# A four-layer fp32 trunk: the two parts of x and h at other SBUF distances from the weights in each feed-forward phase

## The reference, cut to what matters

```python
# x: (1, 256, 1024); DEPTH = 4; D_FF = 2816; all float32
def _swiglu(h, w_gate, w_up, w_down):
    return (jax.nn.silu(h @ w_gate) * (h @ w_up)) @ w_down

for i in range(DEPTH):
    x = x + 0.5 * _swiglu(_rms_norm(x, norm_ffn1[i]), ffn1_w_gate[i], ffn1_w_up[i], ffn1_w_down[i])
    h = _rms_norm(x, norm_mix[i])
    # mixer by i % 3: forgetting attention (layers 0 and 3), a convolution module (1),
    # differential attention (2)
    x = x + y
    x = x + 0.5 * _swiglu(_rms_norm(x, norm_ffn2[i]), ffn2_w_gate[i], ffn2_w_up[i], ffn2_w_down[i])
return x
```

## Time and profile before

| what | value |
|---|---|
| time, median of 2 runs | 1983.55 us (1982.61 to 1984.5) |
| the profiled execution | 1982.23 us |
| its span | 1980.4 us |
| mean granted TensorE clock | 0.997 of 2.4 GHz |
| TensorE matmuls, weight loads | 12558, 12558 |

### The profile page before, as it was taken

The page is one execution under the profiler, slowest core; times in us unless marked ns, Lnnn a source line. Parts: engine busy times, 40 slices in busy tenths (PEclk is TensorE's granted clock), DMA queues, the critical chain, the costliest instruction groups (busy, mean ns, idle before and its releaser), DMA issues.

```text
span 1980.4 us, 29058 instructions
## 1 busy us (share of the span) xinstructions
PE 1948.2 (98%) x12558; PEld 1712.4 (86%) x12558; DVE 1423.8 (72%) x1653; ACT 1044.4 (53%) x1250; POOL 102.0 (5%) x114
## 2 busy tenths in 40 slices
PE   7999999999999998999999999999999999999999
PEld 6888889888888896988888888788888888889887
DVE  7776678875787565876587658887758765778763
ACT  6554556553555344654465455575436544566542
POOL 3000001000200002100100000010000000001000
PEclk9999999999999999999999999999999999999999
DMA  7655435655665683665666553356566656435653
GB/s 239 193 184 182 149 128 157 192 188 187 192 192 180 201 246 89 191 192 188 194 191 192 180 181 128 107 178 192 180 196 191 191 181 193 139 128 171 192 189 107
DMA packets 336365, 350.14 MB, mean 177 GB/s; under 512 B 10077, under 2 KB 331886, under 8 KB 336238
## 3 DMA queue, kind: packets, MB, share of 16 engines
q1 hardware_dynamic: 331742, 343.58, 54.5%
q10 hardware_dynamic: 4496, 4.70, 1.2%
HBM read 346.04 MB, written 2.22 MB: 176 GB/s over the span
## 4 chain that ended last, share of the span: by engine, by line
PE 91%; DVE 4%; ACT 2%; DMA 1%; issue 1%; POOL 1%; ACTq 0%; SPq 0%; DVEq 0%; POOLq 0%
PE banks L1458 49%; PE banks L1463 25%; PE banks L1449 4%; PE banks L1450 4%; PE banks L1451 4%; PE banks L1675 1%; DMA u_away<-sb_u_pad 1%; PE banks L1728 1%; ACT sb_w_high L475 1%; DVE sb_w_low L813 1%; PE banks L1695 1%; PE banks L1712 1%; PE banks L1916 1%; ACT sb_scores L603 0%; DMA sb_raw<-in_ffn_w_gate 0%
## 5 line engine op out<-in xcount | busy, mean ns | idle before, releaser
L813 DVE TENSOR_TENSOR sb_w_low<-sb_raw,sb_w_high 128x2048 fp32r<-128x2048 f32 (+1 forms) x332 | 749.9, 2262 | 211.4 <-ACT sb_w_high L475 210.6
L1458 PE MATMUL banks<-sb_x_both,sb_w_high 128*128 128x512 f32 x2816 | 720.7, 392 | 2.2 <-ACT sb_w_high L475 2.2
L475 ACT ACTIVATE sb_w_high<-sb_raw 128x2048 fp32r<-128x2048 f32 (+1 forms) x332 | 618.5, 1867 | 124.1 <-DMA sb_raw<-in_ffn_w_down 106.6
L1458 PEld LDWEIGHTS banks<-sb_x_both,sb_w_high 128*128 128x128 f32 x2816 | 498.5, 188 | 82.6 <-ACT sb_w_high L475 2.4
L1463 PEld LDWEIGHTS banks<-sb_x_both,sb_w_low 128*128 128x128 f32 x2792 | 386.1, 188 | 35.5
L1463 PE MATMUL banks<-sb_x_both,sb_w_low 128*128 128x256 f32 x2792 | 394.3, 278 | 0.0
L1458 PE MATMUL banks<-sb_h_both,sb_w_high 128*128 128x512 f32 x1408 | 360.1, 394 | 0.0
L1458 PEld LDWEIGHTS banks<-sb_h_both,sb_w_high 128*128 128x128 f32 x1408 | 250.2, 188 | 45.7
L1463 PEld LDWEIGHTS banks<-sb_h_both,sb_w_low 128*128 128x128 f32 x1408 | 190.8, 188 | 17.1
L1463 PE MATMUL banks<-sb_h_both,sb_w_low 128*128 128x256 f32 x1408 | 194.2, 278 | 0.0
L493 ACT ACTIVATE sb_x_both<-sb_xT,sb_vec 128x256 fp32r<-128x256 f32 x96 | 43.3, 500 | 199.5 <-DVE sb_xT L846 175.5
(11 more groups left out here) (232 smaller groups left out, 1931.1 us busy)
## 6 DMA issues: line engine op xcount, KB each, us to landing
sb_raw<-in_ffn_w_gate SPq DMA_DIRECT2D x88, 1024.0 KB, 5.4
sb_raw<-in_ffn_w_up SPq DMA_DIRECT2D x88, 1024.0 KB, 5.4
sb_raw<-in_ffn_w_down SPq DMA_DIRECT2D x64, 1024.0 KB, 5.0
sb_raw<-in_ffn_w_down SPq DMA_DIRECT2D x32, 768.0 KB, 4.3
sb_raw<-in_fox_w_in SPq DMA_DIRECT2D x24, 1024.0 KB, 5.2
sb_raw<-in_conv_w_pw SPq DMA_DIRECT2D x12, 1024.0 KB, 6.2
sb_raw<-in_diff_w_in SPq DMA_DIRECT2D x12, 1024.0 KB, 5.1
sb_raw<-in_fox_w_out SPq DMA_DIRECT2D x8, 1024.0 KB, 4.9
```

Source lines behind the costliest of these rows:

```text
L475: act.activation(slot(w_high, b)[:, 0:width(b)], slot(raw, b)[:, 0:width(b)], ACT.Copy).then_inc(S["high_ready"], 1)
L813: dve.tensor_tensor(slot(w_low, b)[:, 0:width(b)], slot(raw, b)[:, 0:width(b)], slot(w_high, b)[:, 0:width(b)].bitcast(F32), ALU.subtract) ...
L1458: return pe.matmul(pair(bank[at][:, :]), high[:, n * P:(n + 1) * P], m_both, start=first, stop=last, skip_group_check=True)
```

## The change

`x_both` and `shift_x` become one tensor `x_home` of 2 x 8192 + 864 bytes that begins at 114816, at distance 0 from a weight slot. `x_parts(i)` takes the two parts of phase i out of it at `X_PLACE[f]` elements (4 bytes each), f being the number of the feed-forward phase; for a mixer it takes element 16, which is the address of before. `h_both` and `shift_h` become `h_home`, whose start is the address that `h_both` had, with the parts at `H_PLACE[f]` elements from it. All readers and writers of x and h take their views from these functions.

The distances of x's high part from a weight slot, in bytes, are by feed-forward phase 32, 48, 56, 72, 80, 96, 112 and 208 (before: 64 in all). Those of h's, beyond a multiple of 1024, are 32, 48, 80, 96, 16, 160, 224 and 240 (before: 960). The low part follows the high part at 8192 and 22528 bytes, as before. By this layout none of the sixteen is a multiple of 64; two of them, x's 56 and 72, are no multiple of 16. All tensors that stand between x and h (among them the constants, the table `wide` and `gate_parts`) move up by 800 bytes. No instruction is added, removed or moved.

```diff
+X_PLACE = [8, 12, 14, 18, 20, 24, 28, 52]
+H_PLACE = [24, 28, 36, 40, 20, 56, 72, 76]
...
-        sb("shift_x", [P, 16])
-        x_both = sb("x_both", [P, 2, KT, SEQ], F32R)
-        x_high, x_low = x_both[:, 0, :, :], x_both[:, 1, :, :]
+        x_home = sb("x_both", [P, 2 * KT * SEQ + 216], F32R)
+
+        def two_parts(home, tiles, at):
+
+            return home[:, at:at + 2 * tiles * SEQ].rearrange("p (c k n) -> p c k n", c=2, k=tiles)
+
+        def x_parts(i):
+            return two_parts(x_home, KT, X_PLACE[number(i)] if phases[i] == "ffn" else 16)
...
-        sb("shift_h", [P, 200])
         with ExitStack() as during_ffn:
-            h_both = during_ffn.enter_context(nc.sbuf_tensor("sb_h_both", [P, 2, FF_TILES, SEQ], F32R))
+            h_home = during_ffn.enter_context(nc.sbuf_tensor("sb_h_both", [P, 2 * FF_TILES * SEQ + 224], F32R))
...
+        def h_parts(i):
+            return two_parts(h_home, FF_TILES, H_PLACE[number(i)])
...
             def x_highs(i, T):
...
+                x_high = x_parts(i)[:, 0, :, :]
...
             def x_lows(i, T):
...
+                x_high, x_low = x_parts(i)[:, 0, :, :], x_parts(i)[:, 1, :, :]
...
                 def low(p):
                     dve.wait_ge(S["h_high_ready"], PAIRS * f + p + 1)
-                    dve.tensor_tensor(h_both[:, 1, 2 * p:2 * p + 2, :], pair(hidden[:, :]),
-                                      h_both[:, 0, 2 * p:2 * p + 2, :].bitcast(F32),
+                    dve.tensor_tensor(h_low[:, 2 * p:2 * p + 2, :], pair(hidden[:, :]),
+                                      h_high[:, 2 * p:2 * p + 2, :].bitcast(F32),
                                       ALU.subtract).then_inc(S["h_low_ready"], 1)
...
         def _(pe):
+            x_mixer = x_parts(1)
+            x_high, x_low = x_mixer[:, 0, :, :], x_mixer[:, 1, :, :]
...
             def ffn(i):
                 b, f = starts[i], number(i)
+                x_both, h_both = x_parts(i), h_parts(i)
```

More of the change, by code:

```diff
@@ L542, in ffn @@
                 b, f = starts[i], number(i)
+                h_high = h_parts(i)[:, 0, :, :]
                 def upper_half(p, which):
@@ L556, in high @@
                     act.wait_ge(S["hidden_ready"], PAIRS * f + p + 1)
-                    act.activation(h_both[:, 0, 2 * p:2 * p + 2, :], pair(hidden[:, :]), ACT.Copy
+                    act.activation(h_high[:, 2 * p:2 * p + 2, :], pair(hidden[:, :]), ACT.Copy
                                    ).then_inc(S["h_high_ready"], 1)
@@ L959, in ffn @@
                 b, f = starts[i], number(i)
+                h_high, h_low = h_parts(i)[:, 0, :, :], h_parts(i)[:, 1, :, :]
                 def gate(p):
@@ L1589, in very_first_pair @@
                                     for k in ks:
-                                        on_high(at + n, n, low[:, k, :], x_high[:, k, :])
+                                        on_high(at + n, n, low[:, k, :], x_both[:, 0, k, :])
                         wait_block(which)
@@ L1594, in very_first_pair @@
                                 ins = pe.matmul(bank[at + n][:, SEQ:2 * SEQ], low[:, k, n * P:(n + 1) * P],
-                                                x_high[:, k, :], start=False, stop=k == KT - 1, skip_group_check=True)
+                                                x_both[:, 0, k, :], start=False, stop=k == KT - 1, skip_group_check=True)
                         ins.then_inc(S["block_done"], 1)
@@ L1832, in forget_gates @@
                     for k in range(KT):
-                        ins = pe.matmul(pair(bank[6][0:3 * FOX_HEADS, :]), gate_parts[:, k, :], x_both[:, :, k, :],
+                        ins = pe.matmul(pair(bank[6][0:3 * FOX_HEADS, :]), gate_parts[:, k, :], x_mixer[:, :, k, :],
                                         start=k == 0, stop=k == KT - 1)
```

## The result

The changed kernel takes 2014.64 us (median of 2 runs, 2013.58 to 2015.7) against 1983.55 us: ratio 1.015, 95% interval 1.0134 to 1.0166. It is slower by 31 us. The forecast was 2005, in the direction and within the range; its +22 us are some seven tenths of what came.

What follows compares the result with a forecast made beforehand. TensorE's matmul steps were taken to bound the eight feed-forward phases; +22 us for x's and h's distances, 0 for low parts and moved tensors, on 1982.2 us gave 2004, or 2005 on the median; range 1945 to 2060.

Steps and rivals of the forecast that it cites:

- +22 us: Feed-forward phases: predicted extra time from x's and h's new distances from the weights, x 18 us and h 4 us.
- The main term: Feed-forward matmuls: x's and h's new distances from the weights change the ns per pair over 4224 pairs, +22 us.
- The dearer shown level in all phases: Feed-forward phases: every untried distance costs 233.3 ns for `on_both` and 117.8 for `on_high`, 351 ns a pair.
- rival B: Feed-forward phases: off the 64-byte grid is worse, much worse where distances leave 32; +51 us, 2035 us; chance 0.28.
- A: The main forecast: feed-forward pairs lie between 344 and 352 ns, 2005 us in all (1985 to 2023); chance 0.40.
- The argument of a draw at random: Feed-forward phases: x's 344.6 ns is the better of two shown pair levels, so random new places are likelier worse.
- the join that I subtracted: Forget gates: 2 x 113.3 = 226.7 ns taken as two undisturbed joined runs, leaving 6 ns for loading 48 columns.
- Rival C: Feed-forward phases: the 64-byte grid itself makes load and stream collide, so leaving it saves 48 us, 1936 us; chance 0.14.
- Rival D: Feed-forward phases: the change does nothing; only larger distances or those between own parts count; 1984 us within 5; chance 0.18.

## Why the prediction was right, and where it was not

**The bound was read rightly.** From the second phase to the seventh TensorE had no gaps in the x and h parts before and has none after. Of the 33.5 us 29.6 lie in the x and h parts, and all but the 1.2 us of longer waits in the first phase's x part are steps of the same matmuls; nowhere do they wait longer for the writers of x and h, whose own busy time rose by less than 1 us.

**The main term had the right sign and mechanism, and for x the wrong size.** "The dearer shown level in all phases" gave x +18 and h +4. Measured: x +26.0, h +3.6. The step that failed is the ceiling for x: I held the dearer levels of before, 233.3 and 117.8 ns (351 a pair), for the dearest on this ground, and said that the phases would lie between 344 and 352. In their steady series, with 344.6 ns before, those at 32, 48, 80 and 112 bytes do (350 to 351 ns, the last three with x parts 1.8 to 2.0 us dearer). At 96 and 208 a pair takes 353 and 354 ns, at 56 and 72 359 and 360 (239 and 120 to 121.5). The sum had 2.3 us for each phase; 56 and 72 alone bring 10.4 us, of which the run with them on the line took back 6.4, and 96 and 208 bring 6.3. The first phase is 3.5 us up, part of it its own scatter. That h's sum came out to 0.4 us says less than it seems, since its single parts rose by anything from -0.1 to 0.9 us. And the range, 1945 to 2060, was wide enough to hold rival B's 2035 as well: it is the times of the phases that speak for A, not the total.

**The argument of a draw at random held.** x was at the best of four classes; every place of another class, on or off the grid of 64 bytes, was worse. h stood at the second best of the four, and one new place (16 bytes) was level with it.

**Rival B fell.** It wanted the phases at 32, 96, 160 and 224 bytes above 365 ns a pair. In steady series x at 32 takes 233 + 117 = 350 ns, as the eighth phase of the run in reverse order shows best, and at 96 it takes 233 + 120 = 353; h takes 350 to 353 at its four. Its row was misread: the forget gates kept their 2.02 us when their distance became a multiple of 64, and the join that I subtracted costs nothing. Their weights also step by 192 bytes from tile to tile where x steps by 1024, so that these eight matmuls run through four distances modulo 256, before and after, and speak for none. What a load of 48 columns does to its matmul (some 20 ns above the columns) remains unexplained.

**Rival C fell.** No place off the grid of 64 bytes was cheaper for x; and the transposes kept their 108 ns when their distance changed from 32 beyond a multiple of 64 to a multiple of it, so that the number said nothing of distances.

**Rival D fell**: the distance between stream and weights alone, with the same instructions, moved the x part from 121.8 to 127.1 us. With it fell what the prediction drew from the Trainium skill, "TensorE: Matmul & The Clock Gate", Part 2, which says that the load of the next weights takes no read bandwidth from the running matmul. Whether it is read bandwidth that is lost, no run shows. D's guess that the parts' own distance matters was right as a fact (64 bytes there, +2.3 us), but not as a reason for no change, since that distance stayed.

The other page cited is of the Trainium skill too, "SBUF — State Buffer", "Door 1: The DMA port swizzle", with its lines of 16 bytes. The estimate by it was some 4 us for the two places at 56 and 72 bytes; putting them on a line gave 6.4 us. Its count of one more line touched doesn't explain why a rest of 12 costs about 1 us and a rest of 4 or 8 more than 4, though each of them touches 65 lines.

**The mixers** were put at 0 within 2 us and are at +3.7, 2.6 of them in the convolution, whose time scatters by 3 us among executions of one layout. What the prediction left out is that h's place reaches into them: 0.8 us in their first 48 matmuls. The tables' new addresses were not tried apart, but three runs have them with h at its old place, and there the other three mixers together take 0.2 to 0.7 us more than before.

What stays open is the mechanism below the distance: why 256 bytes are the period, why 64 is the good class, and how one series hands its state to the next. The runs show the prices, not the circuit. That the partner of the stream is the weight load is argued from one run, in which weights and operands moved by 32 bytes together and every part from the second phase on had its old time; matmuls without a load beside them were not tried.

## What to carry to other kernels

In a stream of matmuls that each load their own weights, look at the distance from start to start, not at the duration: 344.6 ns a pair where the columns are 320 is a hint that something beside the columns is being paid. The distance in SBUF between the moving operand and the weights, modulo 256 bytes, was worth up to 2.7% of such a stretch (125.1 us against 121.8), and a start 8 bytes off the 16-byte line another 2.5% (3.0 and 3.1 us). A kernel of several equal phases can try eight places in one run, since here each x part from the second phase on repeated to 0.2 us; put the places in another order once to see that it is the place that costs. And look at the matmuls behind the part that was changed, which can take another step with none of their operands moved.

## What the runs showed of the hardware that was not expected

- The price of a place repeats after 256 bytes: 121.8 us at 64, 320 and 832; 124.0 at 128 and 384; 122.5 at 192 and 704; 123.3 to 123.4 at 256 and 512.
- Moving weights and operands together by 32 bytes changes nothing in an x or h part; by 8 bytes it costs 3.1 us in an x part and 0.9 in an h part.
- With the weights on a 16-byte line, x 12 bytes past a line costs about 1 us in an x part over its time at 64 bytes, 4 or 8 bytes past it 4 to 5 us.
- Two runs of 256 columns in one matmul are as fast as one run of 512: 229 ns both.
- The same 256-column matmul has two steady steps, 113.4 and 117.7 ns, and which one it takes depends on what ran before it: a mixer's first 48 take the one or the other by where h stood, and the same series of the third phase takes 0.91 or 0.94 us.
